# A two-layer mixer kernel: the memory branch's queries are turned by a transfer of 16-bit planes, and its scores and values stand later in the order

## The reference

```python
def hybrid_mixer(h, mem, ...):
    proj = h @ w_in
    moba_qkv, fox_qkv, fox_f, pool_u, mem_q, gate_logits = jnp.split(proj, IN_SPLITS, axis=-1)
    ...
    o_m = memory_cross_attention(mem_q, mem, norm_mem, w_mem_kv, mem_q_gain, mem_k_gain)
    branches = jnp.stack([o_a, o_b, o_c, o_m], axis=2)
    y = jnp.einsum('bsnc,ncd->bsnd', branches, w_branch)
    gates = jax.nn.sigmoid(gate_logits.reshape(b, s, N_BRANCH, D_MODEL))
    return jnp.sum(gates * y, axis=2) @ w_out

def memory_cross_attention(q_flat, mem, norm_gain, w_kv, q_gain, k_gain):
    q = rms_norm(to_heads(q_flat, MEM_HEADS, MEM_HEAD_DIM), q_gain)      # 4 heads of 128
    k_m, v_m = jnp.split(rms_norm(mem, norm_gain) @ w_kv, 2, axis=-1)
    k_m = rms_norm(to_heads(k_m, MEM_HEADS, MEM_HEAD_DIM), k_gain)
    v_m = to_heads(v_m, MEM_HEADS, MEM_HEAD_DIM)
    logits = jnp.einsum('bhqd,bhmd->bhqm', q, k_m).astype(jnp.float32) * (MEM_HEAD_DIM ** -0.5)
    p = jax.nn.softmax(logits, axis=-1).astype(v_m.dtype)
    return from_heads(jnp.einsum('bhqm,bhmd->bhqd', p, v_m))
```

## Time and profile before

| | before |
|---|---|
| median of 3 runs | 1324.18 us (1323.96 to 1324.52) |
| the profiled execution | 1324.03 us |
| its span, first to last instruction | 1322.0 us |
| TensorE busy | 1317.1 us, 100% of the span |
| VectorE busy | 932.3 us, 71% |
| ScalarE busy | 689.9 us, 52% |
| GpSimd busy | 289.9 us, 22% |

### The profile page before, as it was taken

How to read it: one execution, slowest core, us unless ns; L and a number is a source line. 1 busy time by engine, 2 the same in 40 slices (tenths; PEclk the granted TensorE clock), 3 DMA queues, 4 the chain that set the end, 5 groups by cost and what they waited for, 6 DMA issues and landing times.

```text
span 1322.0 us, 15770 instructions
## 1 busy us (share of the span) xinstructions
PE 1317.1 (100%) x6094; PEld 1088.3 (82%) x6094; DVE 932.3 (71%) x1174; ACT 689.9 (52%) x957; POOL 289.9 (22%) x282
## 2 busy tenths in 40 slices
PE   9999999999999999999999999999999999999999
PEld 8888888888888888888888888888888878888887
DVE  6566777789987675665475664787999876665653
ACT  6444465554756455444455454556556554645442
POOL 0324312033421002323003230020524110023220
PEclk9999999999999999999999999999999999999999
DMA  8968666568756447776557776555767665577671
GB/s 318 266 209 224 181 226 194 193 183 261 201 180 211 161 152 245 209 221 216 190 191 223 212 223 195 196 166 176 218 223 199 207 198 176 178 220 223 207 215 64
DMA packets 205466, 269.41 MB, mean 204 GB/s; under 512 B 94144, under 2 KB 104272, under 8 KB 205392
## 3 DMA queue, kind: packets, MB, share of 16 engines
q1 hardware_dynamic: 204208, 264.98, 64.7%
q0 software_dynamic: 896, 3.16, 0.7%
q10 hardware_dynamic: 288, 0.27, 0.1%
HBM read 245.30 MB, written 1.06 MB: 186 GB/s over the span
## 4 chain that ended last, share of the span: by engine, by line
PE 99%; DMA 0%; DVE 0%; SPq 0%; issue 0%; DVEq 0%
PE psum L718 24%; PE psum L981 23%; PE psum L745 21%; PE psum L728 12%; PE psum L986 12%; PE psum L939 1%; PE psum L839 1%; PE psum L877 1%; PE psum L943 1%; PE psum L711 1%; PE psum L844 1%; PE psum L886 1%; PE psum L665 0%; PE psum L855 0%; DMA raw<-in_w_ffn_in 0%; PE psum L924 0%
## 5 line engine op out<-in xcount | busy, mean ns | idle before, releaser
L1478 DVE TENSOR_TENSOR ring_lo<-raw,ring_hi 128x1024 fp32r<-128x1024 f32 x459 | 599.7, 1321 | 315.5 <-ACT ring_hi L1052 313.9
L1052 ACT ACTIVATE ring_hi<-raw 128x1024 fp32r<-128x1024 f32 x462 | 480.6, 1047 | 554.0 <-PE psum L728 234.9
L718 PE MATMUL psum<-ring_hi,hT 128*128 128x512 f32 x1376 | 339.9, 389 | 0.0
L718 PEld LDWEIGHTS psum<-ring_hi,hT 128*128 128x128 f32 x1376 | 258.3, 188 | 53.7
L981 PE MATMUL psum<-ring_hi,hT 128*128 128x512 f32 x960 | 240.1, 392 | 0.0
L981 PEld LDWEIGHTS psum<-ring_hi,hT 128*128 128x128 f32 x960 | 178.4, 188 | 38.4 <-issue 1.0
L728 PE MATMUL psum<-ring_lo,hT 128*128 128x512 f32 x704 | 188.7, 390 | 0.0
L1366 POOL COPY planes<-gate 128x1024 uint16<-128x1024 uint16 (+1 forms) x48 | 68.0, 1445 | 456.0 <-DVE gate L1552 456.0
L728 PEld LDWEIGHTS psum<-ring_lo,hT 128*128 128x128 f32 x704 | 131.8, 188 | 27.1
L986 PE MATMUL psum<-ring_lo,hT 128*128 128x512 f32 x480 | 128.3, 389 | 0.0
L745 PE MATMUL psum<-ring_hi,act_hi 128*128 128x512 f32 x352 | 110.4, 389 | 0.0
(11 more groups left out here) (202 smaller groups left out, 1214.0 us busy)
## 6 DMA issues: line engine op xcount, KB each, us to landing
raw<-in_w_ffn_in SPq DMA_DIRECT2D x78, 1024.0 KB, 5.2
raw<-in_w_in SPq DMA_DIRECT2D x64, 1024.0 KB, 5.3
raw<-in_w_ffn_out SPq DMA_DIRECT2D x44, 1024.0 KB, 5.0
raw<-in_w_branch SPq DMA_DIRECT2D x16, 1024.0 KB, 5.3
raw<-in_w_ffn_in SPq DMA_DIRECT2D x18, 512.0 KB, 4.8
raw<-in_w_mem_kv SPq DMA_DIRECT2D x8, 1024.0 KB, 5.1
raw<-in_w_out SPq DMA_DIRECT2D x8, 1024.0 KB, 5.0
forget<-negc_rows POOLq DMA_DIRECT2D x2, 1024.0 KB, 7.7
```

What stands on the lines that cost most here:

```text
L718: pe.matmul(outs[t][:, :], hT[part][:, kc, t * P:(t + 1) * P], w[0][:, kc - first, :], start=kc == 0 and part == 0, stop=False)
L1052: act.activation(unit_out(0, step, k), view, ACT.Copy).then_inc(hi_done.sem, 1)
L1478: dve.tensor_tensor(unit_out(1, step, k), view, unit_out(0, step, k).bitcast(F32), ALU.subtract)\
```

## The change

The memory queries leave TensorE. A fifth job, `QM_ROWS`, joins `turn_rows`, between the memory keys and the probabilities of g = 0 in GpSimd's order, and its DMA transpose stands behind the load of step 16. Since they come out of it already in SBUF, ScalarE now multiplies them in place by the gain, at the start of step 14, in one operation of 128x1024. `scores` 0 moves from the middle of step 13 to the middle of step 14, its exponentials and shares from step 14 to 15, `values` 0 from the end of step 17 to the end of step 19, `values` 1 from the end of step 22 to the end of step 23, and the transposes of the probabilities of g = 0 from behind the load of step 20 to behind that of 21. MOBA's keys are still turned by TensorE, now into banks 4 and 5.

```diff
-        ("PE", _step_of("gate", (1, 0), 1), END, 0), ("ACT", _step_of("gate", (1, 0), 1), END, 0),
+        ("ACT", _step_of("qa"), START, 0),
...
-ROWS_BEHIND = {_step_of("qm", None, 1): 0, _step_of("qc"): 1, _step_of("gate", (3, 1), 1): 2, _step_of("gate", (0, 0), 1): 3}
+ROWS_BEHIND = {_step_of("qm", None, 1): 0, _step_of("gate", (1, 1)): 1, _step_of("qc"): 2, _step_of("gate", (3, 1), 1): 3,
+               _step_of("gate", (0, 0), 1): 4}
...
-TURNED_BEHIND = dict(zip([_step_of("ka"), _step_of("gate", (3, 0), 1)], BY_DMA))
+TURNED_BEHIND = dict(zip([_step_of("ka", None, 1), _step_of("gate", (3, 0), 1)], BY_DMA))
 for g, scores, exps, turned, summed in [
-    (0, _step_of("y", (1, 0)), _step_of("qa"), None, _step_of("gate", (1, 1), 1)),
-    (1, _step_of("gate", (1, 1), 1), _step_of("y", (1, 1)), None, _step_of("qc")),
+    (0, _step_of("qa"), _step_of("qa", None, 1), None, _step_of("y", (1, 1))),
+    (1, _step_of("gate", (1, 1), 1), _step_of("y", (1, 1)), None, _step_of("qc", None, 1)),
...
-            home = pT[:, 0:2, :].rearrange("p b s -> p (b s)") if job == KMEM_ROWS else pool_in[:, :, :].rearrange("p g n -> p (g n)")
+            home = pT[:, 0:2, :].rearrange("p b s -> p (b s)") if job in (KMEM_ROWS, QM_ROWS) else pool_in[:, :, :].rearrange("p g n -> p (g n)")
...
-                    if arg == MOBA:
-                        pe.wait_ge(rotated.sem, rotated.at(L, 2))
-                    if arg == MEM:
-                        pe.wait_ge(split_lo.sem, split_lo.at(L, 2 * SPLITS.index("mixed") + 2))
-                    else:
-                        attended(L, 2 * arg)
-                    pe.wait_ge(taken_dve.sem, taken_dve.at(L, release({MEM: "qm", MOBA: "ka"}[arg])))
-                    i = 0 if arg == MEM else 1
+                    pe.wait_ge(rotated.sem, rotated.at(L, 2))
+                    pe.wait_ge(exp_done.sem, exp_done.at(L, 2))
                     for c in range(BC):
                         for t in range(NT):
                             at = (c % 2) * SEQ + t * P
-                            mm = pe.transpose(bank[4 + 2 * i + c // 2][:, at:at + P], qk[:, i, t, c * P:(c + 1) * P], ident)
+                            mm = pe.transpose(bank[4 + c // 2][:, at:at + P], qk[:, 1, t, c * P:(c + 1) * P], ident)
...
-                    if arg == MEM:
-                        act.wait_ge(qkT_ps.sem, qkT_ps.at(L, 1))
-                        for b in range(2):
-                            last = act.activation(qkT_buf[:, MEM % 2, 0, 2 * b:2 * b + 2, :],
-                                                  bank[4 + b][:, :].rearrange("p (c t) -> p c t", c=2), ACT.Copy,
-                                                  scale=gain(L, HEAD_AT + 2))
...
+                    job, at = (QM_ROWS, 2) if arg == MEM else (QC_ROWS, 0)
+                    act.wait_ge(rows_merged.sem, rows_merged.at(L, job + 1))
+                    columns = qkT_buf[:, arg % 2, 0]
+                    act.activation(columns, columns, ACT.Copy, scale=gain(L, HEAD_AT + at)).then_inc(qT_ready[arg].sem, 1)
...
                 turn_rows(L, KMEM_ROWS, kmem[:, :, :], qkT_buf[:, MEM % 2, 1])
+                pool.wait_ge(taken_dve.sem, taken_dve.at(L, release("qm")))
+                turn_rows(L, QM_ROWS, qk[:, 0], qkT_buf[:, MEM % 2, 0])
                 turned(L, 0)
```

More of the change, by code:

```diff
@@ L349, in build @@
         squares = tally("squares", 2 * len(NORMED))
-        qkT_ps = tally("qkT_ps", 2)
+        qkT_ps = tally("qkT_ps", 1)
         qT_ready = [tally(f"qT_ready{br}", 1) for br in range(3)]
         kT_ready = [tally(f"kT_ready{br}", 1) for br in range(3)]
-        rows_planes = tally("rows_planes", 4)
-        rows_turned = tally("rows_turned", 16 * 4)
-        rows_merged = tally("rows_merged", 4)
+        rows_planes = tally("rows_planes", 5)
+        rows_turned = tally("rows_turned", 16 * 5)
+        rows_merged = tally("rows_merged", 5)
         scores_ready = tally("scores_ready", 6)
@@ L421, in plane_words @@
             return NT * 512
-        KMEM_ROWS, QA_ROWS, QC_ROWS, KC_ROWS = range(4)
+        KMEM_ROWS, QM_ROWS, QA_ROWS, QC_ROWS, KC_ROWS = range(5)
         def row_planes(job):
-            home = pT[:, 0:2, :].rearrange("p b s -> p (b s)") if job == KMEM_ROWS else pool_in[:, :, :].rearrange("p g n -> p (g n)")
+            home = pT[:, 0:2, :].rearrange("p b s -> p (b s)") if job in (KMEM_ROWS, QM_ROWS) else pool_in[:, :, :].rearrange("p g n -> p (g n)")
             return home.bitcast(U16)
@@ L1286, in serve @@
                     else:
[L1288 to L1291, removed]
+                        if kind in ("qa", "qc"):
+                            act.wait_ge(rows_planes.sem, rows_planes.at(L, {"qa": QM_ROWS, "qc": QA_ROWS}[kind] + 1))
+                        elif kind == "kc":
+                            act.wait_ge(qkT_ps.sem, qkT_ps.at(L, 1))
                         dst, heads = HEAD_DST[kind]
@@ L1696, in task @@
                     if arg == MOBA:
[L1697 removed]
+                        dve.wait_ge(qkT_ps.sem, qkT_ps.at(L, 1))
                         for b in range(2):
                             last = dve.tensor_copy(qkT_buf[:, MOBA % 2, 1, 2 * b:2 * b + 2, :],
[L1700 removed]
+                                                   bank[4 + b][:, :].rearrange("p (c t) -> p c t", c=2))
                     else:
```

2 lines of the change are left out of this document (removed).

## The result

The changed kernel takes 1331.71 us (median of 6 runs, 1330.82 to 1333.65) against 1324.18 us before (6 runs beside them, 1323.85 to 1324.52). The ratio is 1.0058, with a 95% interval of 1.0048 to 1.0068: 7.5 us slower. The forecast had the direction, with 1327.0 us, but the time lies above its range, 1323.2 to 1330.5 us. Two of all the executions recorded here, one of the kernel before and one of an experiment's kernel, took 1896.82 and 1763.61 us at a mean granted clock of 0.654 and 0.703, and no comparison uses them.

The account below looks back on a forecast made before the run. TensorE's queue bounds the kernel, every wait in it lost in full. Per layer -0.88 (transposes) + 0.1 (borders) + 2.3 (wait) = +1.5 us; two layers +3.0 on 1324.0 gives 1327.0 us, range 1323.2 to 1330.5.

Parts of the forecast that it names:

- the saving: TensorE's step 12: removing the memory queries' transposes saves 0.88 us a layer, 1.76 us in two layers.
- the load moved to 254.6: SyncE's load of step 16: its issue moves from 253.45 to about 254.3, as VectorE's two units are stretched by 0.84 us.
- the split, the landing, the merge and the gain: Memory queries' turn: split 3.95 us, transpose wait 6.51, merge 3.68, ScalarE's gain 1.14; queries ready at about 266.7.
- the wait: TensorE at `scores` 0: wants the turned queries at 264.44, gets them at about 266.7, waits 2.3 us a layer.
- the quick turn: Rival at the memory queries' turn: landing 4.62 us, wait 0.4 to 1.8 us, total about 1324.5 us; chance 0.27.
- the late landing: Rival at the queries' transpose: landing 8.61 instead of 6.51 us, 2.1 us more a layer, 1331.2 us; chance 0.04.
- the absent wait: Rival at `scores` 0: no wait at all, the chain being shorter than any row says, 1322.4 us; chance 0.03.
- The slow merge: Rival at GpSimd's merge of the queries: 5.20 or 5.83 us instead of 3.68, 1330.0 to 1331.3 us; chance 0.09.
- MOBA's keys ... Net nothing: At MOBA's keys' transposes: a TensorE wait of 0.1 to 0.2 us, offset by a shorter wait at `y (3,0)`.
- VectorE becomes the bound further on: Rival at MOBA's keys or `f`: share 0 and `qa` work in succession cost 0.5 to 1 us a layer; chance 0.05.
- TensorE's clock falls: Rival behind the gap at `scores` 0: clock at 1.2 GHz, 2.7 us more a layer, 1332.4 us; chance 0.05.
- The borders: TensorE's borders between unlike neighbouring tasks after the moves: +0.1 us a layer, ends 0 and 0.2.

Follow-up runs that it names:

- the earlier transpose: Changed kernel with SyncE issuing the memory queries' DMA transpose one load earlier, behind the load of step 15: 1331.85 us, ratio 1.0055.
- second experiment: Changed kernel with its late places kept, but the memory queries turned by TensorE again in step 12, with ScalarE's copies: 1326.51 us, ratio 1.0017.
- first experiment: Changed kernel with `scores` 0 half a step later, at the end of step 14, on TensorE and VectorE: 1325.23 us, ratio 1.0009.
- the best two: Kernel before with `values` 1 behind the keys' transposes, 1324.77 us; changed kernel with `scores` 0 at step 14's end and `values` 1 ahead of them, 1324.82 us.

## Why the prediction was right in direction and wrong in size

**Right.** The bound (TensorE's queue, in which each wait is lost in full), the saving (16 transposes fewer), the load moved to 254.6, the split, the landing, the merge and the gain: the queries are ready 0.6 us later than forecast, TensorE wants them 0.3 us later, and the wait is 2.6 us where the sum had 2.3. Of the rivals, the quick turn, the late landing and the absent wait are refuted by the rows of the turn. The slow merge did not occur here. But what that rival rests on, VectorE's work and GpSimd's copies that hold each other up, shaped the outcome at the keys, and undid the earlier transpose.

**The first step that failed** is "MOBA's keys ... Net nothing". It weighed only the order of TensorE's tasks, and there it was right to 0.6 us (`values` 1 alone moved). It took VectorE's moment at the keys, 319.02, as fixed, though the change moves shares and merges on VectorE and GpSimd too. Measured are waits of 1.4 and 1.6 us, and of 1.0 and 1.4 us with the late places alone (second experiment). About 2 us a layer of VectorE's time there go to GpSimd's merge of g = 1, shown by halving it (1.0 us a layer less) and by moving it (1.7 us at the new place). Before, 1.1 to 1.2 us of that were paid too, behind a pause of VectorE's; in the changed order VectorE has no pause there, and the merge is paid by TensorE. The rival "VectorE becomes the bound further on" named the place and gave 0.5 to 1 us a layer. It had the sign and about half the size, but its reason was share 0 and the work on `qa`, not GpSimd, and the chance of 0.05 was too small for a step that moves so much work of VectorE's.

**The second** is the chance of 0.05 for "TensorE's clock falls". It fell, in both layers, to the level of 1.2 GHz behind the pause. The price was set at a full unit, 2.7 us a layer; it is about 1.4 us for both together in the median and 3.3 us in the profiled execution. I had no row with a pause of 2 us and took the lack of a row for evidence against. The Trainium skill (TensorE: Matmul & The Clock Gate, "What's actually happening") has the half rate as the state after idleness, which this trace bears out, for a shorter pause than I thought enough.

**The sum by what was measured**: -1.8 (transposes) + 5.2 (two waits at `scores` 0) + 1.4 (clock) + 3.0 (two waits at the keys) - 0.4 (the wait at `y (3,0)` that went) = 7.4 us, against 7.5 measured. The last term is 0.14 and 0.22 us from starts; the 0.6 us of the earlier trace rows, which the prediction took for a loss, is PEld's figure, and TensorE's queue lost less. The borders, 0.2 us in the forecast, were not measured. The first experiment checks the sum from the other side: without the wait at `scores` 0 and the clock it is 1325.23 us, and -1.8 + 3.2 - 0.4 = +1.0 us is what it shows over before. Of the 4.7 us by which the forecast was short, the keys are 3.0, the clock 1.4 and the longer wait at `scores` 0 0.6, less the 0.4 at `y (3,0)`: 4.6 us.

**Still open.** Which part of the moved work takes VectorE's pause away ahead of the keys wasn't separated: share 0, `values` 0's copies and the split of g = 1 all moved together. The rows show two candidates just ahead of the keys, the scan stretched by the split (0.8 us) and the remainder of `values` 0 (L1760, 0.68 us), which stood ahead of `scores` 1 before; no experiment moved either alone. Nor was it seen why the clock falls for longer in one execution than in another. No version that computes everything beat the kernel before: the best two, 1324.77 and 1324.82 us, can't be told from it. The one run below it, 1323.27 us, leaves a copy out.

## What to carry to other kernels

When a bound engine's task gets a producer on other engines, ask two things of the gap that may open: how long it is, and whether it is long enough to slow what comes behind it; a few cheap matmuls or a place half a step later avoid the second price. When tasks move, follow each helper engine's copies to what they now run beside: the engine that TensorE waits for can become late by work that isn't in its own queue. And when a reordering takes a wait away, look at the next place where the same two engines meet, before you count it as won: it may have moved there.

## What the runs showed of the hardware that was not expected

- A pause of TensorE of 2.45 us was followed by a granted clock of 0.50 for some 3 us, in both layers; with pauses of 1.6 us in the same place the clock stayed at 1.00, and so did the mean clock of the first experiment, with waits of 1.3 and 1.6 us at the keys. The drop is not the same in every execution: the mean granted clocks of the changed kernel's six are 0.997 to 1.000, and their times spread over 2.8 us, those of the ten of the first experiment over 1.6.
- A VectorE operation on 16 elements a partition took 1.20 us beside a GpSimd copy of 16-bit words and 0.17 us without one, while a reduction over 1024 elements took 1.21 us with the merge beside it (before, 311.41) and 1.20 us with almost none of it (after, 314.02).
- A merge of four GpSimd copies took 3.96 us at one moment and 6.09 us when it began 2.4 us sooner. The landing of a transpose of 512 KB of planes took 4.53 us with no load in front of it, and 6.66 us 0.9 us behind a load of 1 MB; SyncE's queue was held by it for 1.32 and 4.56 us.
